# Two-block transformer kernel on one core: four taps of the first convolution done before the attention's scores, its channel mean inside the attention, its norm in chunks

## The chip, the cores and the metric

The kernel runs on one core of one Trainium2 chip. The metric is the device time of one execution in microseconds. Each kernel is timed in several executions, and the median of them is given. One further execution was recorded by the hardware profiler, and all rows below come from that one.

## The reference, cut to what matters

The program computes two transformer blocks over 256 tokens of width 1024, batch 1, in fp32. The first block begins with a mixer: an attention with 8 heads of 64 beside a convolution branch over 512 channels. The change is in that convolution branch.

```python
def conformer_conv(a, g, conv_w, conv_b, ln_g, ln_b):
    u = a * jax.nn.sigmoid(g)
    u = depthwise_conv(u, conv_w, width=31, padding=15) + conv_b   # 31 taps for each channel
    u = layernorm(u, ln_g, ln_b)                                   # over the 512 channels
    return jax.nn.silu(u)

att = dilated_sliding_attention(q, k, v)                           # 8 heads
h = h + concatenate([att, conv], axis=-1) @ w_out                  # 1024 x 1024
```

Behind it, and untouched by the change, come a cross attention, an MLP, and the two layers of the second block with a mixture of experts at the end.

## The kernel before, in words

Everything is written per engine, with semaphores between the engines. `after("name", i)` gives the semaphore value at which a named instruction has finished, and `do(..., "name", i)` marks it. Each engine runs its own list in order, so an instruction that waits holds up everything behind it on that engine.

Matrix products are made of fp32r pieces. Every fp32 operand is split into a high part (a rounded copy) and a low part (the rest), and `matmul3` issues three matmuls for each product (lines 538, 539 and 540 of the profile). Weights come in slots of 1 MB: SyncE loads a slot (three raw buffers), ScalarE writes its high part in two halves (`high`, L1461), VectorE its low part in two halves (`low`, L1983), and TensorE then uses it. There are two split buffers, so `high` of slot j waits until TensorE is done with slot j-2, and the load of slot j waits until `low` of slot j-3 is done.

The first attention is a software pipeline over steps s = 0 to 9. In step s TensorE computes the scores of head s (L758), transposes the probabilities of head s-1 (L652), multiplies those of head s-2 by the values (L672), and then does a piece of other work, `between(s)`. That piece is `cross_values(s)` for s below 8: 12 matmuls of 512 columns for the cross attention's values. VectorE in step s scales and masks the scores (L2267), takes the maximum (L2270), waits for ScalarE's exponentials, takes a reciprocal, does `low` in the even steps, and splits the attention output of a pair of heads (`outs1`, L1988 and L1990) in steps 3, 5, 7 and 9.

VectorE also computes the convolution, tap by tap, in the gaps. The 512 channels lie as four chunks of 128 x 256 in the tile C (all in the tile that the profile calls arena). `conv_taps(n)` does n pairs: a pair is one tap for two chunks, so two instructions of 128x256 (L2188). There are 62 pairs in all; the calls stop by themselves once 62 are done. 38 of them are done before the call `conv_taps(1)` that stands just ahead of the attention's loop on VectorE.

After the last tap, TensorE sums C over the channels by matmuls with a matrix of ones (`mean_over_channels`, L768; four fp32 matmuls, which the profile counts as eight), VectorE subtracts the mean (`conv_mean`, L2242), ScalarE squares (L1616), TensorE sums the squares (L768 again), VectorE scales (L2247), ScalarE takes the root (L1618), VectorE takes the reciprocal and multiplies (L2252, L2254), ScalarE applies SiLU (L1622), and VectorE splits the result (`conv_split`, L1988 and L1990).

The product with `w_out` has four slots, called wout0 to wout3 here. The first two need only the attention's four 128-row pieces of the joined input (k = 0 to 3), the last two the convolution's (k = 4 to 7). The order on TensorE after the attention is: channel mean, half of wout0, sum of squares, the other half of wout0, wout1, then a wait for the whole convolution result (`convT`), then wout2 and wout3. Transposes of the new residual and the cross attention's query projection follow.

Of the kernel before, what the change touches and what calls it, by code (L numbers as in the profile page):

```python
# [137 lines left out]
def program(nc, A, out, points, stop):  # L138
    ctx = ExitStack()
    with ctx:  # L140
# [180 lines left out]
        def col(name, i=0):  # L321
            return COL[:, COLS[name] + i:COLS[name] + i + 1]
# [55 lines left out]
        def after(*name):  # L378

            key, n = points.get(name, ("pe", 1))  # L380
            return sems[key], n
# [139 lines left out]
        with nc.Block() as block:  # L521
# [3 lines left out]
            def _(pe):  # L525
# [16 lines left out]
                def open_bank(*name):  # L542

                    k = len(order)
                    if k >= 4:
                        pe.wait_ge(*after("read", *order[k - 4]))
                    order.append(name)
                    bank_of[name] = RING_BANK[k % 4]
                    return RING_BANK[k % 4]
# [183 lines left out]
                features_out("xk", MT, "xk", 3)  # L733
                pe.wait_ge(*after("read", "qkT", 3))
                pe.wait_ge(*after("read", "v", 0, 1))
                cross_slot = {}

                def cross_values(s):
                    if s >= 8:
                        return  # L740
                    i, r, t = s // 4, s // 2 % 2, s % 2
                    if t == 0:
                        cross_slot[i, r] = weights("xv")
                    j, w = cross_slot[i, r]
                    ps = open_bank("xv", i, t) if r == 0 else bank_of["xv", i, t]
                    for k in range(4):
                        mm = matmul3(ps[:, :], lambda z: MT[:, z, 4 * r + k, t * P:(t + 1) * P],
                                     lambda z: w[:, z, k, :], r == 0 and k == 0, r == 1 and k == 3)
                    if r == 1:
                        mm.then_inc(*cpe.mark("filled", "xv", i, t))  # L750
                        cpe.also("slot", j)
                    elif t == 1:
                        mm.then_inc(*cpe.mark("slot", j))
# [7 lines left out]

                attention(0, AH, scores1, pair_outs("att_o", (), V), between=cross_values)

                def mean_over_channels(name, need, src):
                    pe.wait_ge(*after(need))
                    ps = open_bank(name)
                    for k in range(4):
                        mm = pe.matmul(ps[:, 0:S], ones, src[:, k, :], start=(k == 0), stop=(k == 3))  # L768
                    mm.then_inc(*cpe.mark("filled", name))

                for c in range(2):
                    for t in range(TT):
                        bank_of[("wout", c, t)] = banks[2 * t + c]
# [6 lines left out]
                                         lambda z: w[:, z, k % 4, :], first and k == ks[0], last and k == ks[-1])  # L780
                    return mm

                mean_over_channels("cmean", "conv", C)
                pe.wait_ge(*after("scores_read", AH - 1))
                pe.wait_ge(*after("pt_copied", AH - 1))
                pe.wait_ge(*after("read", "att_o", 3))
# [3 lines left out]
                mixed_rows(0, w, (0, 1, 2, 3), (1,), first=True).then_inc(*cpe.mark("slot", j))  # L790
                j, w = weights("wout")
                mixed_rows(1, w, (0, 1, 2, 3), (0, 1), first=True).then_inc(*cpe.mark("slot", j))
                pe.wait_ge(*after("convT"))
                for c in range(2):
                    j, w = weights("wout")
                    for t in range(TT):
                        if c == 1 and t == 1:
                            first_half_raw(2)
                        mixed_rows(c, w, (4, 5, 6, 7), (t,), last=True).then_inc(*cpe.mark("filled", "wout", c, t))
                    cpe.also("slot", j)  # L800

                features_out_raw("xq", 2, "xq", 0)
# [614 lines left out]
            def _(act):  # L1417
# [20 lines left out]
                def do(ins, *name):  # L1438
                    ins.then_inc(*cact.mark(*name))
# [176 lines left out]
                do(act.activation(SIG[:, :, :], C[:, :, :], ACT.Square), "csq")  # L1616
                act.wait_ge(*after("read", "cvar"))
                do(act.activation(U[:, 0, 0:S], U[:, 0, 0:S], ACT.Sqrt), "csd")  # L1618
                high(1)
                act.wait_ge(*after("cnormed"))  # L1620
                for i in range(4):
                    do(act.activation(C[:, i, :], C[:, i, :], ACT.Silu, bias=col("conv_ln_b", i),  # L1622
                                      scale=col("conv_ln_g", i)), "csilu")
                high(1)
                sum_deferred(2, 2, 0)
                def query(i):
# [333 lines left out]
            def _(dve):  # L1960
                def do(ins, *name):
                    ins.then_inc(*cdve.mark(*name))
# [287 lines left out]
                def conv_scaled():  # L2250
                    dve.wait_ge(*after("csd"))
                    do(dve.reciprocal(U[:, 1, 0:S], U[:, 0, 0:S]))  # L2252
                    own()
                    do(dve.tensor_tensor(C[:, :, :], C[:, :, :],  # L2254
                                         U[:, 1, 0:S].unsqueeze(1).broadcast_to([P, 4, S]), ALU.mult), "cnormed")

                def conv_split():
                    dve.wait_ge(*after("csilu"))
                    split(lambda z: CAT[:, z, 4:8, :], C[:, :, :], "convT")

                conv_taps(1)
                for s in range(AH + 2):
                    if s < AH:
                        dve.wait_ge(*after("scores", s))
# [8 lines left out]
                        do(dve.reciprocal(RDEN[:, s % 3, :], DEN[:, s % 3, :]), "rden", s)  # L2273
                    if s in (0, 2, 4, 6, 8):
                        low(1)
                    if s >= 3 and s % 2:
                        outs1(s - 2)
                    conv_taps(2 if s % 2 else 1)
                assert taps_done == [TAPS, TAPS]
                conv_mean()  # L2280
                conv_variance()
                conv_scaled()
                low(1)
# [609 lines left out]
```

## Time and profile before

| | before |
|---|---|
| median of 3 timed runs | 1460.79 us (1459.87 to 1461.65) |
| the profiled execution's own time | 1454.22 us |
| span in the profile | 1452.2 us |
| mean granted TensorE clock | 0.991 |
| TensorE matmul busy | 1387.2 us (96%) |
| VectorE busy | 1080.0 us (74%) |
| ScalarE busy | 840.2 us (58%) |

Times in the rows are counted from the start of the span. Positions such as "at 157.80" are such times. The profiled execution took 2.0 us more than its span, and it was shorter than the median of the timed runs by 6.6 us.

### The profile page before, as it was taken

What the parts mean: (1) busy time and instruction counts of PE and PEld (TensorE: products, weight loads), DVE (VectorE), ACT (ScalarE), POOL (GpSimd) and SP (SyncE); (2) the same over time, 40 slices, a digit from 0 to 9 for tenths busy, and PEclk for the clock granted to TensorE, in tenths of its full rate; (3) what the DMA queues carried; (4) which work ended last, traced back from release to release, by engine and by line L of the source; (5) the groups of instructions that cost most, each with busy time, mean ns of one, the idle gap of its engine ahead of it and who ended that gap; (6) DMA issues with size and microseconds to landing.
All of it is one profiled execution on the core that took longest, in us unless ns stands there. A gap on an engine that the chain in (4) does not pass through costs nothing.

```text
span 1452.2 us, 21919 instructions
## 1 busy us (share of the span) xinstructions
PE 1387.2 (96%) x8180; PEld 1212.3 (83%) x8180; DVE 1080.0 (74%) x1560; ACT 840.2 (58%) x1173; POOL 56.2 (4%) x60
## 2 busy tenths in 40 slices
PE   6999899999999989999999998999999999999997
PEld 6786697999988977899999997777888888888885
DVE  4988666655658887655556888677898898898896
ACT  4546453443436844444334484446788787787784
POOL 0000000000001130000000012010000000000000
PEclk9999999999999999999999999998999999999999
DMA  8642343565654501455555440119998998998982
GB/s 301 207 146 87 100 148 103 173 200 178 197 178 132 175 30 49 126 174 190 188 181 177 144 153 30 59 44 350 362 385 301 336 355 297 358 336 306 378 314 111
DMA packets 162963, 292.75 MB, mean 202 GB/s; under 512 B 6832, under 2 KB 78924, under 8 KB 162764
## 3 DMA queue, kind: packets, MB, share of 16 engines
q1 hardware_dynamic: 162336, 291.08, 57.9%
q8 instruction: 50, 0.82, 0.2%
q10 hardware_dynamic: 556, 0.67, 0.1%
q14 instruction: 21, 0.17, 0.0%
HBM read 290.69 MB, written 1.05 MB: 201 GB/s over the span
## 4 chain that ended last, share of the span: by engine, by line
PE 85%; DVE 9%; ACT 3%; issue 1%; SPq 1%; DMA 1%; POOL 0%; DVEq 0%; ACTq 0%; POOLq 0%
PE bank L538 24%; PE bank L540 24%; PE bank L539 24%; DVE weights_split L1983 3%; PE bank L1232 2%; PE bank L1035 1%; PE bank L1307 1%; PE bank L1041 1%; PE bank L1026 1%; ACT weights_split L1461 1%; PE bank L672 1%; PE bank L652 1%; PE bank L1053 1%; PE bank L1284 1%; SPq L1378 1%
## 5 line engine op out<-in xcount | busy, mean ns | idle before, releaser
L1983 DVE TENSOR_TENSOR weights_split<-weights,weights_split 128x1024 fp32r<-128x1024 f32 (+4 forms) x266 | 304.3, 1186 | 168.6 <-ACT weights_split L1461 168.4
L1461 ACT ACTIVATE weights_split<-weights 128x1024 fp32r<-128x1024 f32 (+4 forms) x266 | 258.4, 1022 | 265.0 <-PE bank L540 260.2
L538 PE MATMUL bank<-features_split,weights_split 128*128 128x256 f32 x912 | 262.6, 288 | 15.9 <-DVE weights_split L1983 5.5
L539 PE MATMUL bank<-features_split,weights_split 128*128 128x256 f32 x912 | 260.0, 285 | 0.0
L540 PE MATMUL bank<-features_split,weights_split 128*128 128x256 f32 x912 | 259.9, 285 | 0.0
L538 PE MATMUL bank<-weights_split,features_split 128*128 128x512 f32 (+3 forms) x560 | 216.9, 387 | 8.6 <-DVE features_split L1990 3.9
L540 PE MATMUL bank<-weights_split,features_split 128*128 128x512 f32 (+3 forms) x560 | 212.9, 380 | 0.0
L539 PE MATMUL bank<-weights_split,features_split 128*128 128x512 f32 (+3 forms) x560 | 212.7, 380 | 0.0
L538 PEld LDWEIGHTS bank<-features_split,weights_split 128*128 128x128 f32 x912 | 176.9, 194 | 19.8 <-DVE weights_split L1983 7.2
L539 PEld LDWEIGHTS bank<-features_split,weights_split 128*128 128x128 f32 x912 | 177.1, 194 | 0.5
L540 PEld LDWEIGHTS bank<-features_split,weights_split 128*128 128x128 f32 x912 | 176.9, 194 | 0.0
L538 PE MATMUL bank<-weights_split,hidden_split 128*128 128x512 f32 x376 | 149.0, 396 | 0.0
L540 PE MATMUL bank<-weights_split,hidden_split 128*128 128x512 f32 x376 | 146.7, 390 | 0.0
L539 PE MATMUL bank<-weights_split,hidden_split 128*128 128x512 f32 x376 | 146.5, 390 | 0.0
L538 PEld LDWEIGHTS bank<-weights_split,features_split 128*128 128x128 f32 x560 | 106.0, 189 | 27.3 <-DVE features_split L1990 4.7
L540 PEld LDWEIGHTS bank<-weights_split,features_split 128*128 128x128 f32 x560 | 105.7, 189 | 17.8
L539 PEld LDWEIGHTS bank<-weights_split,features_split 128*128 128x128 f32 x560 | 106.0, 189 | 16.7
L2807 DVE TENSOR_TENSOR weights_split<-weights,weights_split 128x1024 fp32r<-128x1024 f32 x96 | 114.8, 1221 | 3.4 <-ACT weights_split L1848 2.5
L1848 ACT ACTIVATE weights_split<-weights 128x1024 fp32r<-128x1024 f32 x96 | 100.5, 1058 | 22.7 <-PE bank L540 22.0
L538 PEld LDWEIGHTS bank<-weights_split,hidden_split 128*128 128x128 f32 x376 | 70.7, 188 | 16.3 <-issue 1.5
L540 PEld LDWEIGHTS bank<-weights_split,hidden_split 128*128 128x128 f32 x376 | 70.6, 188 | 15.3
L539 PEld LDWEIGHTS bank<-weights_split,hidden_split 128*128 128x128 f32 x376 | 70.7, 188 | 13.6
(387 smaller groups left out, 2250.5 us busy)
## 6 DMA issues: line engine op xcount, KB each, us to landing
weights<-in_moe_gate_dram SPq DMA_DIRECT2D x26, 1024.0 KB, 6.7
weights<-in_moe_up_dram SPq DMA_DIRECT2D x24, 1024.0 KB, 7.0
weights<-in_moe_down_dram SPq DMA_DIRECT2D x24, 1024.0 KB, 7.1
weights<-in_w_in_dram SPq DMA_DIRECT2D x20, 1024.0 KB, 5.1
weights<-in_w_up_dram SPq DMA_DIRECT2D x16, 1024.0 KB, 5.2
weights<-in_w_down_dram SPq DMA_DIRECT2D x16, 1024.0 KB, 4.9
weights<-in_w_out_dram SPq DMA_DIRECT2D x12, 1024.0 KB, 5.0
weights<-in_ffn_gate_dram SPq DMA_DIRECT2D x11, 1024.0 KB, 5.3
```

The source lines that it names most:

```text
L538: pe.matmul(ps, lhs(0), rhs(0), start=start, stop=False, skip_group_check=shared)
L539: pe.matmul(ps, lhs(0), rhs(1), start=False, stop=False, skip_group_check=shared)
L540: return pe.matmul(ps, lhs(1), rhs(0), start=False, stop=stop, skip_group_check=shared)
L652: mm = pe.transpose(ps[:, at:at + P], pr[:, kt * P:(kt + 1) * P], ident)
L672: mm = pe.matmul(ps[o:o + HD, first:S], v[:, kt, h * HD:(h + 1) * HD], flat(pt)[:, kt * S:(kt + 1) * S - first], start=(kt == 0), stop=(kt ...
L1026: mm = pe.matmul(inplace(ps[:, i * P:(i + 1) * P].unsqueeze(1), lev), LT[:, p, :], chosen(DI, p, 1, lev), start=True, stop=True)
L1035: mm = pe.matmul(ps[:, i * P:(i + 1) * P], DITC[:, p, :], PM[:, p, :], start=True, stop=True)
L1232: mm = pe.matmul(ps[:, k * P:(k + 1) * P], XS[:, z, t, f * P:(f + 1) * P], GSEL[:, t, :], start=(t == 0), stop=(t == TT - 1))
L1461: do(act.activation(split_flat(j)[:, 0, part], raw_flat(j)[:, part], ACT.Copy), "hi", j, b)
L1848: do(act.activation(split_flat(j)[:, 0, part], raw_flat(j)[:, part], ACT.Copy), "hi_item", s, b)
L1983: do(dve.tensor_tensor(split_flat(j)[:, 1, part], raw_flat(j)[:, part], split_flat(j)[:, 0, part].bitcast(F32), ALU.subtract), "lo", j)
L2807: do(dve.tensor_tensor(split_flat(j)[:, 1, part], raw_flat(j)[:, part], split_flat(j)[:, 0, part].bitcast(F32), ALU.subtract), "lo_item", ...
```

## The change

Four things are changed.

1. VectorE does four pairs of taps instead of one ahead of the attention loop, and two instead of one at the end of step 0. The last pair of taps now falls in step 7; before, steps 8 and 9 had one and two pairs.
2. TensorE's channel mean moves from behind the attention into step 8, behind the value product of head 6. VectorE's `conv_mean` moves into step 9, ahead of the split of the last pair of heads.
3. ScalarE gets one more activation, a SiLU of one column, behind the root. VectorE's multiplication by the reciprocal is done in four instructions of 128x256 instead of one of 128x1024, and each SiLU waits for its own chunk.
4. The split of the convolution result is done in two halves, and TensorE waits for the first half ahead of k = 4, 5 and for the second ahead of k = 6, 7.

```diff
+                def mean_over_channels(name, need, src):
+                    pe.wait_ge(*after(need))
+                    ps = open_bank(name)
+                    for k in range(4):
+                        mm = pe.matmul(ps[:, 0:S], ones, src[:, k, :], start=(k == 0), stop=(k == 3))
+                    mm.then_inc(*cpe.mark("filled", name))
+
                 def cross_values(s):
+                    if s == 8:
+                        mean_over_channels("cmean", "conv", C)
                     if s >= 8:
                         return
...
-                mean_over_channels("cmean", "conv", C)
                 pe.wait_ge(*after("scores_read", AH - 1))
...
-                pe.wait_ge(*after("convT"))
                 for c in range(2):
                     j, w = weights("wout")
                     for t in range(TT):
                         if c == 1 and t == 1:
                             first_half_raw(2)
-                        mixed_rows(c, w, (4, 5, 6, 7), (t,), last=True).then_inc(*cpe.mark("filled", "wout", c, t))
+                        pe.wait_ge(*after("convT", 0))
+                        mixed_rows(c, w, (4, 5), (t,))
+                        pe.wait_ge(*after("convT", 1))
+                        mixed_rows(c, w, (6, 7), (t,), last=True).then_inc(*cpe.mark("filled", "wout", c, t))
...
                 do(act.activation(U[:, 0, 0:S], U[:, 0, 0:S], ACT.Sqrt), "csd")
+                do(act.activation(SM[:, 15, 0:1], NHALF[:, 0:1], ACT.Silu))
                 high(1)
-                act.wait_ge(*after("cnormed"))
                 for i in range(4):
+                    act.wait_ge(*after("cnormed", i))
                     do(act.activation(C[:, i, :], C[:, i, :], ACT.Silu, bias=col("conv_ln_b", i),
-                                      scale=col("conv_ln_g", i)), "csilu")
+                                      scale=col("conv_ln_g", i)), "csilu", i)
...
-                    do(dve.tensor_tensor(C[:, :, :], C[:, :, :],
-                                         U[:, 1, 0:S].unsqueeze(1).broadcast_to([P, 4, S]), ALU.mult), "cnormed")
+                    for i in range(4):
+                        do(dve.tensor_tensor(C[:, i, :], C[:, i, :], U[:, 1, 0:S], ALU.mult), "cnormed", i)
 
                 def conv_split():
-                    dve.wait_ge(*after("csilu"))
-                    split(lambda z: CAT[:, z, 4:8, :], C[:, :, :], "convT")
-
-                conv_taps(1)
+                    for p in range(2):
+                        dve.wait_ge(*after("csilu", 2 * p + 1))
+                        split(lambda z: CAT[:, z, 4 + 2 * p:6 + 2 * p, :], C[:, 2 * p:2 * p + 2, :], "convT", p)
+
+                conv_taps(4)
                 for s in range(AH + 2):
...
+                    if s == AH + 1:
+                        conv_mean()
                     if s >= 3 and s % 2:
                         outs1(s - 2)
-                    conv_taps(2 if s % 2 else 1)
+                    conv_taps(2 if s % 2 or s == 0 else 1)
                 assert taps_done == [TAPS, TAPS]
-                conv_mean()
                 conv_variance()
```

## Rows read from the trace of the kernel before

**Rows 1.** The page: TensorE's busy time, and engines' shares of the chain that ended last.

```profile
PE 1387.2 (96%) x8180; PEld 1212.3 (83%) x8180; DVE 1080.0 (74%) x1560; ACT 840.2 (58%) x1173; POOL 56.2 (4%) x60
...
PE 85%; DVE 9%; ACT 3%; issue 1%; SPq 1%; DMA 1%; POOL 0%; DVEq 0%; ACTq 0%; POOLq 0%
```

**Rows 2.** TensorE's waits from 100 to 230: in total, times, longest, us.

```profile
PE bank L768 <- DVE arena L2188: 3.1, 1, 3.1
PE bank L538 <- DVE features_split L1990: 2.4, 1, 2.4
...
PE bank L672 <- ACT probsT L1529: 1.2, 1, 1.2
```

**Rows 3.** The chain that ended last, 104 to 200: start, length, what.

```profile
151.13 1.07 ACT weights_split L1461
152.22 2.36 DVE weights_split L1983 x2
154.59 0.79 DVE arena L2188 x2
155.38 0.34 DVE features_split L1988
155.75 0.42 DVE features_split L1990
156.17 1.59 DVE arena L2188 x4
157.80 2.88 PE bank L768 x8
...
164.18 1.73 PE bank L768 x8
...
169.04 2.01 ACT weights_split L1461 x2
171.07 1.28 ACT L1622
172.37 2.09 ACT arena L1622 x4
...
175.21 1.24 DVE features_split L1990
176.49 0.50 PE bank L538
```

**Rows 4.** VectorE in order of time; in brackets the idle time before.

```profile
100.85 4.05 DVE L2188 SCALAR_TENSOR_TENSOR arena<-arena,vector_cols 128x256 f32<-128x256 f32 x10
107.68 0.69 DVE L2267 SCALAR_TENSOR_TENSOR probs<-bank,shape_table 128x512 f32<-128x512 f32 x1 [2.77 <-PE bank L758]
...
114.68 0.68 DVE L2267 SCALAR_TENSOR_TENSOR probs<-bank,shape_table 128x512 f32<-128x512 f32 x1
...
160.72 1.23 DVE L2242 SCALAR_TENSOR_TENSOR arena<-bank,arena 128x1024 f32<-128x1024 f32 x1 [2.97 <-PE bank L768]
...
166.85 1.75 DVE L2252 RECIPROCAL arena<-arena 128x256 f32<-128x256 f32 x1 [0.48 <-ACT arena L1618]
```

**Rows 5.** TensorE in order of time, same columns.

```profile
118.40 0.66 PE L652 MATMUL bank<-shape_table,probs 128*128 128x128 f32 x4 [1.23 <-ACT probs L1535]
...
153.67 1.08 PE L672 MATMUL bank<-probsT,arena 128*64 128x256 f32 x4 [1.19 <-ACT probsT L1529]
```

**Rows 6.** Stretches: length, busy time of PE, PEld, DVE, ACT, POOL; granted clock, DMA share, GB/s.

```profile
158.90:162.10 3.20, 3.20 (x9) 2.55 (x8) 1.23 (x1) 0.12 (x1) 0.00 (x0) 0.50 0.03 12
...
165.90:168.72 2.82, 2.82 (x14) 2.29 (x13) 2.26 (x3) 0.42 (x1) 0.00 (x0) 1.00 0.00 0
173.90:176.49 2.59, 0.21 (x2) 0.01 (x1) 1.98 (x3) 2.44 (x4) 0.00 (x0) 1.00 0.99 341
```

**Rows 7.** ScalarE in order of time, around the root.

```profile
163.06 1.28 ACT L1618 ACT_TABLE_LOAD   x1
166.40 0.42 ACT L1618 ACTIVATE arena<-arena 128x256 f32<-128x256 f32 x1 [2.06 <-DVE arena L2247]
```

More of the change, by code:

```diff
@@ L762, in _ @@
                 attention(0, AH, scores1, pair_outs("att_o", (), V), between=cross_values)
[L764 to L769, printed above, removed]
                 for c in range(2):
```

## The prediction

> **What bounds the kernel now.** I read the page first, then TensorE's waits, then the chain that ended last, and then each engine in order of time around the change. TensorE's matmuls are busy for 96% of the span and 85% of the chain lies on TensorE [rows 1], so an edit pays only by the idle time of TensorE that it removes, or by a stretch that TensorE runs at a lower clock. The list of its waits names what is to be had where the convolution meets the attention: 3.1 us ahead of the channel mean (L768, waiting for the last tap), 2.4 us ahead of the second half of the `w_out` product (L538, waiting for the split of the convolution result), and 1.2 us ahead of the last value product (L672) [rows 2]. The chain shows the same place: it leaves TensorE at 151.13, goes over ScalarE's and VectorE's weight split, taps, a split, taps, comes back at 157.80, and leaves again from 169.04 to 176.49 [rows 3]. Third, the clock: from 158.90 to 162.10 it is granted at 0.50, that is 1.2 GHz in place of 2.4, after TensorE had idled 1.2 us, worked about 1 us and idled 3 us; the idle 2.4 us ahead of 176.49 left it at 1.00 [rows 2, 5, 6].
>
> **The moved taps.** A pair costs 0.79 us (two instructions) [rows 3]. Three pairs go ahead of the loop: 3 x 0.79 = 2.37 us. VectorE idles 2.77 us there for the first scores [rows 4], so they are hidden, with 0.40 us left. If that cover were gone they would cost what lies above it, 2.37 us at most. The fourth pair goes to the end of step 0, directly ahead of the scaling of the second scores at 114.68, which waits for nothing [rows 4]. That scaling releases the maximum, the exponentials and the probabilities for which TensorE idles 1.23 us at 118.40 [rows 5]. So it is on the path: plus 0.79. From there to the last value products TensorE has no wait in its list, so it carries the 0.79 along (ScalarE's `high`, whose slot TensorE frees, too) until 151.13 becomes 151.92. In exchange step 7 ends after one pair in place of two: 62 - 42 pairs are left for the loop, steps 0 to 6 take 3+3+2+3+2+3+2 = 18, and step 7 the last two. The last tap ends at 151.65, about where the first of step 7's two final pairs, moved by 0.79, lies.
>
> **The chain from 151.13 to the first `w_out` product.** Before: `low` until 154.59, one pair 0.79, the split of the last heads 0.34 + 0.42, two pairs 1.59, and TensorE's mean 2.88: the product starts at 160.68 [rows 3]. After: `low` ends 0.79 later, 155.38. Then `conv_mean`, 1.23 us alone [rows 4], about 1.15 as a step of a full queue: 156.55. Then the split of the last heads, 0.8: 157.35, and the product starts at 157.4. TensorE's mean must be ready by 155.38: its value product of head 6 ended at 153.67 - 1.19 = 152.5 [rows 5], now 153.3; the taps are done since 151.65; the mean takes 1.73 at full clock [rows 3], until 155.0. That leaves 0.4 us. The last value product (1.08 [rows 5]) then runs until 156.1, and TensorE idles 1.3 us in place of 1.2 + 3.1. Gain: 160.68 - 157.4 = 3.3 us, with the 0.79 already paid.
>
> **The clock.** Half of wout0, the sum of squares and the other half took until 168.72, 8.04 us. At full clock the second half is 2.82 us [rows 6], the first then 2.9, the sum of squares 1.73 [rows 3]: 7.45. I take full clock, since the longest idle time is now 1.3 us, and 2.4 us left the clock alone [rows 2, 6]. The gain is 0.6 us; were the clock at half as before, it would be nothing. wout0 is free at 164.9.
>
> **The second wait.** TensorE then has wout1, 168.72 to 176.49 - 2.38 = 174.1, 5.4 us: until 170.3. Everything for wout2 must be there by then. ScalarE's `high` starts 0.32 us after the slot is free [rows 3]: 165.2 to 167.25. The SiLU's table load, 1.28 us now between `high` and SiLU [rows 3], moves up behind the root, as the root's own load already lies ahead of its wait [rows 7]. The root ends near 163.05, load and one-column activation at about 164.6 (no row has that activation; between nothing and the 0.42 of the root [rows 7], I take 0.2): hidden in the wait for wout0's slot. If not hidden, at most 1.7 us. The reciprocal (1.75 [rows 4]) ends at 164.85. Four multiplications of 128x256: the nearest row is the pair's 0.79, 0.40 each and 1.6 in all, against 1.23 for one of a 128x1024 instruction [rows 3, 4]; bounds 1.2 and 1.9; they end at 166.5. Then `low` of wout2, 2.36 us [rows 3], until 168.9. The first two SiLUs, 0.52 each [rows 3], are done at 168.3. The first half split: a copy and a subtraction of 128x512. The subtraction lies between half of 1.24 and 1.24 [rows 3], and I take the 0.69 of the 128x512 instruction at 107.68 [rows 4]; the copy lies between 0.37 and 0.75 (172.37 + 2.09 to 175.21 is the whole one [rows 3]), and I take 0.42: 170.05. TensorE wants it at 170.3, so 0.2 to 0.3 us are left, and with both upper bounds it would wait 0.6 us. The second half is done near 171.2 and is wanted 6 matmuls later, at 171.7. So the wait of 2.4 us goes. wout3's `high` starts when wout1 is free, its `low` ends near 174.1, and it is wanted at 175.8. VectorE adds the first `w_out` result about 1 us later than TensorE makes it, but TensorE needs that only behind wout3's first three quarters.
>
> The Trainium skill ("ScalarE: Activation LUTs", "What ACT_TABLE_LOAD costs") gives 1.28 us for the load and another 1.38 us of drain with each switch. By its 2.66 us the one-column SiLU would end near 165.9 and `high` start 0.7 us later, which would leave TensorE waiting some 0.2 us and make the gain 6.0 us. The row with the load is followed 0.02 us after its end by the SiLU [rows 3], so I see no such drain in this trace and count none.
>
> **Sum.** 3.3 + 0.6 + 2.4 = 6.3, less 0.1 for the handovers: 6.2 us. No DMA is added or moved by itself; SyncE's loads follow VectorE's `low`, which comes earlier or keeps its distance to TensorE. Behind 176.49 all engines follow TensorE, and no wait for a load of weights is in its list [rows 2], so the 6.2 us should last. Span 1452.2 - 6.2 = 1446.0, own time of a profiled execution 1454.22 - 6.2 = 1448.0. The median of the runs stands 6.6 us above the profiled execution, and I take the same difference off it: 1460.79 - 6.2 = 1454.6 us, 0.42% less.
>
> **The rivals.**
> 1. *The path is as above* (72%). 1454.6 us; with the bounds above and the clock of other executions, 1453.4 to 1456.5. It may be that the timed executions of before don't all have the half-clock stretch: then the mean cost 1.73 and not 2.88 there, the 0.6 isn't gained either, and 6.2 - 1.15 - 0.6 = 4.5 us are left: 1456.3.
> 2. *The clock falls somewhere else* (13%). The idle time at 118.40 grows from 1.23 to 2.0 us, and about 1 us lies shortly ahead of it [rows 5]; and all later stalls come 6 us sooner, so the clock may fall at others. A stretch like the one at 158.90 costs half of its 3.2 us [rows 6], 1.6 us. One or two of them: 1456.2 to 1457.8. Against it: only the 3 us stall shows a fall here. The Trainium skill ("TensorE: Matmul & The Clock Gate", "Part 1: The HAM clock gate") says that an idle array is put at half rate and that sustained work lifts it; where in time the fall comes it leaves open, and this trace agrees with one fall and one return.
> 3. *The handover isn't gained* (11%): the mean is moved, but the halves come late, or later stages swallow the time. If the second wait stays and only the first goes, 3.3 + 0.6 = 3.9 us; if a later stage bound by something other than TensorE takes back half of all, 3.1 us; with one clock fall on top, 1.5 to 2.3 us: 1458.5 to 1460. For it: two margins of 0.2 to 0.4 us. Against it: missing them costs tenths.
> 4. *Slower* (4%). After the longer idle time at 118.40 the clock goes to half and the attention's mix of transposes and short products doesn't lift it. Each 3.2 us at half cost 1.6 us [rows 6], so to lose 6.2 + 2.9 us it must stay at half for 18 us, to about 137; until 151 it would cost 16 us: 1460.8 - 6.2 + 16 = 1470.6. Against it: the same mix kept the clock at 1.00 behind two idle times of 1.2 us, and the fall at 158.90 was over in 3.2 us.
>
> **How the numbers follow.** About 0.2% (2.9 us) is what a measurement of this kernel can tell from no change. Case 1, case 2 but for a tail, and a small part of case 3 give faster by more than that: 85%. Most of case 3 and the tail of case 2 give within 0.2%: 11%. Case 4 gives slower: 4%. The range reaches from 1452.8 (a clock fall fewer downstream, 1.6 us) to 1457.8 (case 2's end).
>
> **What the profile of the changed kernel would show.** VectorE's idle time ahead of 107.7 is 0.4 us in place of 2.77. TensorE's idle time at the second transposes is 2.0 us. The mean (L768's eight) starts directly behind the value product of head 6, near 153.3, and takes 1.7 us. The 3.1 us wait is gone, and one of about 1.3 us ends with L1990 ahead of the first `w_out` product, near 157.4. The clock is 1.00 from 150 to 176. The SiLU's table load stands near 163, ahead of `high`. The second half of the product starts near 170.3 without a wait. The prediction is wrong if the second half waits for the first split by a microsecond or more, if the clock falls between 118 and 165, or if the distance between the two traces shrinks behind 176.

## The result, and the profile after

The changed kernel took 1451.6 us in the median of 8 runs (1449.08 to 1457.93), the kernel before 1460.76 us in the same comparison (1459.87 to 1463.63). The ratio is 0.9934, with an interval from 0.9917 to 0.9952: faster by 9.2 us, 0.6%. The forecast was faster by 6.2 us, 1454.6, with a range from 1452.8 to 1457.8. So the direction was right, and the time lies 1.2 us below the range.

The profiled execution of the changed kernel has a span of 1449.0 us, only 3.2 us less than the 1452.2 of before. So the two profiles differ by 3.2, the medians by 9.2, and the forecast said 6.2. Most of this section and the experiments are about these three numbers.

TensorE's waits in the changed kernel, from 90 to 235 (in total, times, longest):

```profile
PE bank L652 <- ACT probs L1538: 3.0, 2, 2.0
PE bank L538 <- DVE features_split L1994: 2.9, 2, 1.5
PE bank L652 <- DVE probs L2105: 1.9, 2, 1.1
```

The waits of 3.1 us (mean) and 1.2 us (last value product) of [rows 2] are gone. The 2.4 us ahead of the second half are gone too. The two waits for a split that the second row counts are one of 1.5 us near 229, which the kernel before has as well (near 232), and a new one of 1.35 us ahead of the first `w_out` product, for the split of the last heads. TensorE in order of time shows it, with the idle time in brackets:

```profile
120.95 0.66 PE L652 MATMUL bank<-shape_table,probs 128*128 128x128 f32 x4 [2.02 <-ACT probs L1538]
121.53 1.96 PE L672 MATMUL bank<-probsT,arena 128*64 128x256 f32 x4
...
156.54 1.99 PE L740 MATMUL bank<-arena,shape_table 128*128 128x256 f32 x8
158.47 1.08 PE L672 MATMUL bank<-probsT,arena 128*64 128x256 f32 x4
160.90 0.47 PE L538 MATMUL bank<-weights_split,features_split 128*128 128x512 f32 x1 [1.35 <-DVE features_split L1994]
...
163.74 1.89 PE L740 MATMUL bank<-arena,shape_table 128*128 128x256 f32 x8
```

The idle time at the second transposes is 2.02 us, against 1.23 in [rows 5]: the pair at the end of step 0. The mean stands behind the value product of head 6 and holds TensorE for 1.9 us (156.54 to 158.47); in [rows 3] its own length was 2.88, here it is 1.99. No wait lies between 160.90 and the second half, which starts at 173.68.

VectorE and ScalarE around the root, in order of time:

```profile
103.79 5.23 DVE L2192 SCALAR_TENSOR_TENSOR arena<-arena,vector_cols 128x256 f32<-128x256 f32 x13
109.43 0.69 DVE L2272 SCALAR_TENSOR_TENSOR probs<-bank,shape_table 128x512 f32<-128x512 f32 x1 [0.41 <-PE bank L767]
...
158.63 1.22 DVE L2246 SCALAR_TENSOR_TENSOR arena<-bank,arena 128x1024 f32<-128x1024 f32 x1
...
168.37 1.44 DVE L2259 TENSOR_TENSOR arena<-arena 128x256 f32<-128x256 f32 x4
169.72 2.36 DVE L1987 TENSOR_TENSOR weights_split<-weights,weights_split 128x1024 fp32r<-128x1024 f32 x2
171.99 0.43 DVE L1992 CAST features_split<-arena 128x512 fp32r<-128x512 f32 x1
172.45 0.69 DVE L1994 TENSOR_TENSOR features_split<-arena,features_split 128x512 fp32r<-128x512 f32 x1
```

```profile
166.13 0.42 ACT L1621 ACTIVATE arena<-arena 128x256 f32<-128x256 f32 x1 [3.89 <-DVE arena L2251]
166.57 1.28 ACT L1622 ACT_TABLE_LOAD   x1
167.86 0.20 ACT L1622 ACTIVATE small<-minus_half 128x1 f32<-128x1 f32 x1
168.50 2.01 ACT L1464 ACTIVATE weights_split<-weights 128x1024 fp32r<-128x1024 f32 x2 [0.43 <-PE bank L540]
170.42 2.06 ACT L1626 ACTIVATE arena<-arena,vector_cols 128x256 f32<-128x256 f32 x4
```

The idle time ahead of the first scores fell from 2.77 us [rows 4] to 0.41. The table load stands ahead of the weight split, and 0.43 us are left behind it. The first half split ends at 173.1, 0.5 us before TensorE takes it. VectorE's subtraction of the mean (158.63) begins 0.1 us behind the end of TensorE's mean (156.54 + 1.99 = 158.53).

So why only 3.2 us between the two profiles? The stage from the first scores to the second half lasted 69.98 us before (106.51 to 176.49) and 65.41 after (108.27 to 173.68). That is 4.6 us less, not 6.2, and the stage began 1.8 us later, in code that the change hardly touches. Each row below gives a stretch, its length, the busy times of TensorE (matmuls, weight loads), VectorE, ScalarE and GpSimd, and then the granted clock (third number from the end). After:

```profile
108.27:173.68 65.41, 61.02 (x258) 42.78 (x257) 51.45 (x97) 42.00 (x83) 0.00 (x0) 0.97 0.25 82
...
150.00:173.68 23.68, 22.33 (x100) 16.76 (x99) 16.29 (x29) 14.29 (x23) 0.00 (x0) 1.00 0.29 91
```

and three stretches of 10 us that were at 1.00 in the first profile of before. The last row is that profile's own 120 to 130:

```profile
10.00:20.00 10.00, 4.88 (x26) 4.91 (x27) 6.42 (x10) 6.50 (x10) 0.70 (x1) 0.66 1.06 410
...
60.00:70.00 10.00, 7.43 (x36) 5.80 (x35) 10.00 (x16) 4.55 (x6) 0.00 (x0) 0.85 0.49 158
...
120.00:130.00 10.00, 9.05 (x33) 5.69 (x34) 8.52 (x17) 6.05 (x13) 0.00 (x0) 0.83 0.22 66
...
120.00:130.00 10.00, 10.00 (x44) 6.94 (x44) 8.90 (x20) 6.67 (x18) 0.00 (x0) 1.00 0.34 106
```

In this execution the clock fell to 1.2 GHz near 10, near 65, and near 120, behind the longer idle time at the second transposes, but not between 150 and 174. Below, such a stretch at 1.2 GHz is called a fall. The fall near 120 costs the missing 1.6 us of the stage: the four value matmuls at 121.53 took 1.96 us in place of 1.08, and those behind it were slow too. The falls ahead of the stage cost less: the clock was at 0.94 over those 108 us, against 1.00 over the 107 us of before, and the stage began only 1.8 us later.

### The profile page after: what moved, and what is told of

It is laid out like the page before. It is cut to its first block, busy times and chain, and to the rows that moved or that the text cites. A ratio compares the mean times of both kernels' runs of the same rounds, so it can differ in the third digit from the quotient of the medians.

```text
span 1449.0 us, 21926 instructions
## 1 busy us (share of the span) xinstructions
PE 1389.6 (96%) x8180; PEld 1214.3 (84%) x8180; DVE 1080.0 (75%) x1565; ACT 840.2 (58%) x1174; POOL 56.1 (4%) x60
## 4 chain that ended last, share of the span: by engine, by line
PE 86%; DVE 9%; ACT 3%; issue 1%; DMA 0%; POOL 0%; DVEq 0%; SPq 0%; ACTq 0%
PE bank L538 25%; PE bank L540 24%; PE bank L539 24%; DVE weights_split L1987 3%; PE bank L1235 2%; PE bank L1038 1%; PE bank L1310 1%; PE bank L1044 1%; PE bank L1029 1%; ACT weights_split L1464 1%; PE bank L672 1%; PE bank L652 1%; PE bank L1056 1%; PE bank L1287 1%; DVE arena L2557 1%
```

## The experiments

"Theory A" in the expectations is that of the forecast: three handovers on TensorE's path, each worth what its rows say, and the clock drawn anew in each execution. "Stage" is the time from the first scores (the first matmul from `arena`, 64*128) to the first matmul of the second half. The runs of before_filled_stall, before_delay_5p5, delay_5p5_again and no_early_table were made on another chip than those of the other experiments. The kernel before had a median of 1460.8 us there, and of 1461.3 and 1461.2 us in the two comparisons on the other chip.

| kernel | timed median (runs) | ratio, interval | mean clock of the timed runs | stage in its profile | clock in the stage |
|---|---|---|---|---|---|
| before, in the three comparisons of the experiments | 1461.3 (110) | | 0.9830 | 69.98; 70.01 | 0.98; 0.98 |
| changed | 1451.6 (8) | 0.9934, 0.9917 to 0.9952 | 0.9869 | 65.41 | 0.97 |
| after_again | 1453.01 (12) | 0.9952, 0.9935 to 0.9969 | 0.9852 | 63.82 | 1.00 |
| norm_edits_only | 1463.0 (12) | 1.0012, 0.9990 to 1.0033 | 0.9800 | 67.46 | 0.97 |
| taps_mean_only | 1462.4 (12) | 0.9997, 0.9974 to 1.0019 | 0.9821 | 69.31 | 0.95 |
| delay_2p7 | 1456.56 (12) | 0.9984, 0.9955 to 1.0013 | 0.9840 | 66.54 | 1.00 |
| delay_5p5 | 1467.09 (12) | 1.0032, 1.0008 to 1.0057 | 0.9805 | 70.86 | 0.98 |
| delay_5p5_again | 1461.44 (12) | 1.0009, 0.9989 to 1.0029 | 0.9848 | 69.25 | 1.00 |
| no_step0_pair | 1452.54 (8) | 0.9944, 0.9925 to 0.9963 | 0.9852 | 63.03 | 1.00 |
| first_heads_first | 1452.35 (11) | 0.9944, 0.9925 to 0.9963 | 0.9835 | 61.63 | 1.00 |
| before_filled_stall | 1459.58 (12) | 0.9994, 0.9975 to 1.0013 | 0.9838 | 68.30 | 1.00 |
| before_delay_5p5 | 1462.5 (12) | 1.0017, 0.9998 to 1.0035 | 0.9842 | 72.90 | 0.98 |
| no_early_table | 1455.36 (12) | 0.9958, 0.9941 to 0.9974 | 0.9853 | 64.67 | 1.00 |

**before_again.** No edit.

> The kernel before, unchanged, to see what a usual execution of it looks like: its timed runs stand 6.6 us above the one profiled execution. Theory A (the granted clock): the new profile has more stretches at 1.2 GHz than the first one, its mean granted clock is nearer 0.985 than 0.991, and its span is near 1458 us, with the same waits ahead of the channel mean (3 us) and the second half of the w_out product (2.4 us). Theory B (something else in the path): the clock is about 0.991 again, and a wait or a start-up stretch is longer. Timed ratio to before: 1.000 within 0.2%.

The median was 1461.62 us (12 runs, ratio 0.9995). The span was 1457.9 at a mean clock of 0.986, so theory A's picture held: the first profile of before (1452.2 at 0.991) was one of the quick executions. The stage is the same to 0.03 us, with the same waits. What differs lies behind it, in the clock. From 920 to 950, in the first profile of before and then in this one:

```profile
920.00:950.00 30.00, 28.47 (x209) 24.63 (x208) 19.97 (x42) 12.97 (x26) 2.66 (x2) 1.00 0.26 89
```

```profile
106.61:176.62 70.01, 61.12 (x258) 42.98 (x257) 53.31 (x97) 43.66 (x84) 0.00 (x0) 0.98 0.27 88
920.00:950.00 30.00, 28.47 (x203) 25.49 (x203) 17.34 (x39) 12.18 (x27) 1.33 (x1) 0.89 0.20 71
```

**after_again.** No edit.

> The changed kernel, unchanged, beside the kernel before on the same chip. Theory A: again some 8 to 9 us below before (ratio 0.994), of which about 6 us lie between the first scores and the second half of the w_out product and the rest in clock stretches elsewhere, which differ from execution to execution by several us. Theory B: the same difference in every execution, and a stage behind 200 us that is shorter by 3 us at the same granted clock.

In this profile no fall lies in the stage, and the stage lasts 63.82 us: 6.2 us less than before, to the tenth what the sum said. The span is 1457.9 all the same, for the clock was at half for more than half of the 30 us from 920 to 950:

```profile
106.62:170.44 63.82, 59.42 (x258) 41.94 (x257) 51.29 (x97) 41.85 (x83) 0.00 (x0) 1.00 0.25 84
...
920.00:950.00 30.00, 28.47 (x164) 24.39 (x163) 14.15 (x32) 9.08 (x19) 1.33 (x1) 0.72 0.20 71
```

The median is 8.3 us below before, as theory A said. Theory B (a later stage shorter at the same clock) finds nothing: the rest of the program, from the second half on, took 1275.7 and 1281.3 us in the two profiles of before and 1275.3 and 1287.5 in those of the changed kernel. The time lost in it to the clock (length times one less granted clock, summed over stretches of 10 us) was 11.9, 18.3, 11.7 and 26.5 us, in the same order.

**norm_edits_only.** The early table load, the chunks and the halves, without the moved taps and mean:

```diff
-                    if s == 8:
-                        mean_over_channels("cmean", "conv", C)
...
+                mean_over_channels("cmean", "conv", C)
                 pe.wait_ge(*after("scores_read", AH - 1))
...
-                conv_taps(4)
+                conv_taps(1)
...
-                    if s == AH + 1:
-                        conv_mean()
...
-                    conv_taps(2 if s % 2 or s == 0 else 1)
+                    conv_taps(2 if s % 2 else 1)
                 assert taps_done == [TAPS, TAPS]
+                conv_mean()
```

> Only the early SiLU table load, the chunked multiplication, and the split in halves; taps and mean as before. Theory A (two separate handovers): the 2.4 us wait ahead of the second half goes, the 3.1 us wait stays: 2 to 2.6 us faster than before, 1458.3. Rival (the clock decides): with the 3 us wait still there the half-clock stretch stays, but removing the second wait also saves one fall in executions in which it starts one, then up to 4 us. Rival (no gain): the wait stays at 1 us or more since the table load isn't hidden: 1 us or less.

The stage lasted 67.46 us, 2.5 less; the 3.1 us wait and a fall at 158 stayed. The wait ahead of the second half is gone from the list (the 1.5 us are the one far behind it, of which before has its own):

```profile
PE bank L740 <- DVE arena L2191: 3.1, 1, 3.1
PE bank L652 <- ACT probs L1537: 2.3, 2, 1.2
...
PE bank L538 <- DVE features_split L1993: 1.5, 1, 1.5
```

But the timed median, forecast at 1458.3, is no better than before: 1463.0. Its mean clock is the lowest of all, 0.980.

**taps_mean_only.** The other two parts:

```diff
-                        pe.wait_ge(*after("convT", 0))
-                        mixed_rows(c, w, (4, 5), (t,))
                         pe.wait_ge(*after("convT", 1))
-                        mixed_rows(c, w, (6, 7), (t,), last=True)...
+                        mixed_rows(c, w, (4, 5, 6, 7), (t,), last=True)...
...
-                do(act.activation(SM[:, 15, 0:1], NHALF[:, 0:1], ACT.Silu))
...
```

The multiplication is one instruction again, every SiLU waits for it, and the split is one piece.

> Only the moved taps and the channel mean in step 8; norm, SiLU and split as before. Theory A: the first handover gives 3.3 us and the clock at the mean 0.6 us, and the second wait of 2.4 us stays: 3.9 us faster than before, 1456.9. Rival (the clock decides): it gives nearly all of the change, 6 to 9 us, since the stall of 3 us is what lets the clock fall in this stage, and the other edits give nearly nothing.

The first handover goes and the wait of 2.5 us stays. The stage came out at 69.31. The clock was at half in two places where it isn't in before:

```profile
118.20:125.00 6.80, 4.78 (x14) 2.68 (x13) 5.74 (x14) 5.76 (x14) 0.00 (x0) 0.66 0.33 127
176.20:179.60 3.40, 1.93 (x6) 1.63 (x7) 3.37 (x4) 1.23 (x2) 0.00 (x0) 0.83 0.54 190
```

```profile
177.67 0.47 PE L538 MATMUL bank<-weights_split,features_split 128*128 128x512 f32 x1 [2.48 <-DVE features_split L1991]
```

The first lasts from 120 to 127, 6.8 us, as long as two of the falls elsewhere (3.4 us each), and costs the stage some 3.3 us. The second begins near 178.4, behind the 2.48 us wait, and so lies outside the stage. With the first taken out the stage is 66.0 us, 2.3 less than the 68.3 of before without its fall. The rows gave 2.15: 3.3 less the 1.15 that the fall had added to the mean.

The rival, that this part alone gives nearly all, is refuted by the median, 1462.4; so is theory A's 1456.9. By the medians neither part alone gives anything, and both together 8 to 9 us. By the stages without falls they are 2.5 and 2.3 us, and both together 4.5. That called for the next four.

**delay_2p7 and delay_5p5.** Half, or all, of wout1's products computed once more (the expectation below says a quarter, but wout1 has 24 matmuls and takes 5.4 us):

```diff
+                mixed_rows(1, w, (0, 1, 2, 3), (0,), first=True, last=True)     # delay_2p7; (0, 1) in delay_5p5
                 mixed_rows(1, w, (0, 1, 2, 3), (0, 1), first=True).then_inc(*cpe.mark("slot", j))
```

> The changed kernel with 12 matmuls of 512 columns more (a quarter of wout1's products is computed twice), so that TensorE works 2.73 us longer ahead of the second half and everything behind comes later, with no stall added. Theory A (the time lost at 1.2 GHz is drawn anew in each execution and has nothing to do with where the stage ends): 2.7 us slower than the changed kernel, 1455.2. Theory C (the place of the later stalls in time decides how many falls there are): a difference that isn't 2.7 us, between 0 and 7, and a mean granted clock that differs from the changed kernel's 0.986 by 0.003 or more.

> The same with 24 matmuls, 5.46 us, so that the later stages start nearly where they start in the kernel before. Theory A: 5.5 us slower than the changed kernel, 1458.0, still 3 us faster than before, since this stage's own clock falls stay away. Theory C: equal to before, 1461, with the mean granted clock of before, 0.982 to 0.983.

The stages: 66.54 without a fall, 2.72 more than 63.82, and 70.86 with one. The medians: 3.6 us and 14.1 us above after_again. The first is within 1 us of theory A (its mean clock, 0.9840, is 0.002 below the changed kernel's, where theory C asked for 0.003), the second is not: 5.5 us of work cost 14. Theory C's numbers for it (1461, a clock of 0.982 to 0.983) are missed too: 1467.1 at 0.9805. Three of delay_2p7's runs took 1469 us, so its mean lies further off than its median.

**delay_5p5_again.** The same kernel once more, in another comparison and on the other chip.

> The same kernel as delay_5p5, in another job. It came out 14 us above the changed kernel where 5.5 us of work were added. If the excess belongs to this kernel (theory C), it is there again: 1465 to 1469. If it belongs to the job (the phase in which its executions happened to start), the median is nearer 1458 and the mean clock nearer 0.986.

Now 1461.4 at a mean clock of 0.985, where it had been 1467.1 at 0.9805. Neither forecast fits: it lies between them. Of the 8.6 us beyond the added work 3 were there again, so more than half of the excess does not belong to the kernel. Whether it belongs to the chip or to the draw of the clock can't be told from these runs; the kernel before had nearly the same median on both chips.

**no_step0_pair.**

```diff
-                    conv_taps(2 if s % 2 or s == 0 else 1)
+                    conv_taps(2 if s % 2 else 1)
```

> The changed kernel without the pair at the end of step 0. Theory A: TensorE's idle time ahead of the second transposes is 1.23 us again, the stage from the first scores to the second half lasts 63.0 us in place of 63.8, and no fall of the clock comes in the attention: 0.8 us faster than the changed kernel, up to 1.5 with the falls saved, 1451 to 1451.7. Rival: the pair's cost was hidden, no difference, stage 63.8.

The stage lasts 63.03 us, 0.79 less, and the wait at the second transposes is 1.2 us again. The median shows nothing of it (1452.54 against 1453.01 and 1451.6).

**first_heads_first.** The edit of no_step0_pair, and

```diff
-                pe.wait_ge(*after("read", "att_o", 3))
                 j, w = weights("wout")
-                mixed_rows(0, w, (0, 1, 2, 3), (0,), first=True)
+                mixed_rows(0, w, (0, 1, 2), (0,), first=True)
+                pe.wait_ge(*after("read", "att_o", 3))
+                mixed_rows(0, w, (3,), (0,))
```

> The same, and the first w_out product begins with the rows of heads 0 to 5, and waits for the last pair of heads only ahead of its last quarter. Theory A: the 1.35 us wait ahead of the first product goes, the stage lasts 61.7 us, 2.1 us less than in the changed kernel: 1450.4. Rival: the second half then waits for the split of the convolution result (0.5 us of margin in the changed kernel) and 0.5 us or more of it comes back.

The stage lasts 61.63 us, 2.2 less than in the changed kernel, and of the waits between 90 and 180 these are left:

```profile
PE bank L652 <- ACT probs L1539: 2.3, 2, 1.2
PE bank L730 <- ACT arena L1516: 1.3, 1, 1.3
```

It has the shortest path of all. Its median, forecast at 1450.4, is level with the changed kernel's (1452.35 against 1451.6 and 1453.01), at a lower mean clock (0.9835 against 0.9869 and 0.9852).

**before_filled_stall.** In the kernel before, ahead of the wait for the last tap:

```diff
                 def mean_over_channels(name, need, src):
-                    pe.wait_ge(*after(need))
                     ps = open_bank(name)
+                    for _ in range(6 if name == "cmean" else 0):
+                        pe.matmul(ps[:, 0:S], ones, upper_ones, start=True, stop=True)
+                    pe.wait_ge(*after(need))
```

> The kernel before with six fp32 matmuls of 256 columns on the constant tables (2.6 us, into the bank that the channel mean opens anyway) ahead of the wait for the last tap, so that TensorE isn't idle there; the wait's end doesn't move. Theory A (the 3 us stall is what lets the clock fall): no half-rate stretch at 156, the stage from the first scores to the second half lasts 68.3 us in place of 70.0, and the median is 1.7 us below before, 1459.6. Rival: the clock falls there all the same, stage 70.0. Theory C (later falls follow from where the later stages lie): the stage as in A, but a median off by several us either way.

```profile
156.93 2.86 PE L767 MATMUL bank<-shape_table 128*128 128x256 f32 x12
160.05 1.99 PE L770 MATMUL bank<-arena,shape_table 128*128 128x256 f32 x8 [0.27 <-DVE arena L2190]
...
177.07 0.79 PE L538 MATMUL bank<-weights_split,features_split 128*128 128x512 f32 x1 [2.38 <-DVE features_split L1992]
```

```profile
150.00:170.00 20.00, 18.54 (x83) 14.14 (x81) 13.20 (x24) 8.60 (x15) 0.00 (x0) 1.00 0.28 104
174.40:177.80 3.40, 1.02 (x4) 0.63 (x3) 2.70 (x3) 2.52 (x4) 0.00 (x0) 0.84 0.88 304
```

The idle time is gone (0.27 us are left of 3.05), the clock stays up through the mean, and the stage lasts 68.30 us: 1.7 us less for work whose result is overwritten. So the stall let the clock fall, and the fall cost 1.7 us. All four profiles that have this stall have the fall behind it, and this one has neither.

But here the clock fell at the next idle time, the 2.38 us ahead of the second half (its first matmul takes 0.79 us, against 0.50 in [rows 3]), which in both profiles of before had left it alone. That fall lies just behind the end of the stage. The cross attention's first transposes that wait (L652) stand 46.6 to 46.8 us behind the start of the second half in every profile without a fall there. Here it is 48.2 us, and 48.3 in taps_mean_only, where the clock fell behind the same wait. So from the first scores to those transposes before_filled_stall gains only 0.3 us (116.5 against 116.7), and the changed kernel 6.3 (110.4). The median says the same: 0.9994.

The two handovers may therefore not be independent. Where the clock had fallen at 158, the wait of 2.4 us left it alone (2 of 2 profiles); where it had not, it fell there (2 of 2). Only both edits together remove both. That the second fall comes because the first is gone is argued from four profiles and not shown.

**before_delay_5p5.** The 24 extra matmuls in the kernel before.

> The kernel before with 24 more matmuls in wout1 (5.46 us). In it, the second half already waits 2.4 us for the convolution result, so 2.4 us of the delay are hidden: the stage should last 73.1 us. Theory A: 3.1 us slower than before, 1464.4. Theory C: off from that by several us, with the mean granted clock off from 0.983 by the matching amount (0.001 of clock stood for 1.1 us over the runs so far).

The stage lasts 72.90 us, 2.9 more: of 5.5 us of added work, 2.4 went into the wait ahead of the second half, which is gone from its list. The median is 1.7 us above before; theory A said 3.1.

**no_early_table.** The changed kernel without the line with the one-column SiLU.

> The changed kernel without the one-column SiLU, so that the table load (1.28 us) lies between the weight split and the first SiLU again. Theory A: the margin of 0.5 us ahead of the second half is used up and TensorE waits 0.8 us, so the stage lasts 64.6 us in place of 63.8; the median 0.8 us above the changed kernel, which the runs can't tell from the clock's spread. Rival: the load stays hidden behind VectorE's weight split, stage 63.8.

```profile
167.46 1.28 ACT L1625 ACT_TABLE_LOAD   x1
168.76 2.08 ACT L1625 ACTIVATE arena<-arena,vector_cols 128x256 f32<-128x256 f32 x4
```

```profile
171.19 0.47 PE L538 MATMUL bank<-weights_split,features_split 128*128 128x512 f32 x1 [0.69 <-DVE features_split L1993]
```

TensorE waits 0.69 us ahead of the second half, and the stage lasts 64.67 us, 0.85 more. So the margin of 0.5 us was real, and the early load is worth what the load exceeds it by. The median is 1455.36, 2.4 us above after_again's and 3.8 above the changed kernel's first, of which the stage explains 0.85; as the expectation said, the runs don't resolve that.

## Where the prediction was right, and where it was wrong

**The path was right, term by term.** With the stage as the measure, and the one profile of the changed kernel without a fall in it:

- All in all, 6.2 us: 70.0 to 63.82. As predicted.
- The moved taps: three pairs hidden with 0.40 us left (0.41), the fourth 0.79 us on the path. Taking it away gave 0.79.
- The first handover: the product starts 51.03 us behind the first scores in after_again (157.65 less 106.62). Predicted were 157.4 less 106.51, 50.9.
- The clock at the mean: 1.7 us, of which 1.15 was counted in the mean's 2.88 and 0.6 apart. The filled stall gave 1.7 within the stage.
- TensorE's mean: it took 1.99 us at full clock and not 1.73, so of the 0.4 us of margin ahead of VectorE's subtraction 0.1 was left.
- The second handover: 2.4 predicted, 2.5 when made alone.
- The table load: hidden. The Trainium skill ("ScalarE: Activation LUTs", "What ACT_TABLE_LOAD costs") has 1.28 us for the load and 1.38 of drain. The row at 166.57 agrees with the first, and the SiLU at 167.86 stands 0.01 us behind the load's end, so no drain is seen. The margin at the second half was 0.5 us, not 0.2 to 0.3: the four multiplications took 1.44 us, and I had 1.6.

**The step that failed is the last of the sum:** "I take the same difference off it". It takes the path's 6.2 us off the median, as if the clock outside the stage were the same for both kernels. The term that was mis-sized is this clock: the sum puts it at nothing, and the range at one fall of 1.6 us. The timed runs of the changed kernel had a mean clock of 0.9869 (0.9852 in after_again), those of before 0.9830. Worked out below, the 0.0039 between them go with 4.0 us, of which the forecast had the 1.7 of the fall at 158. And the fixed distance of 6.6 us between the profiled execution and the median isn't there: the profiled execution lay 1.7 us below the median in before_again, 0.4 below for the changed kernel, and 7.0 above in after_again. The 6.6 us were mostly clock: 0.991 in the first profile of before, 0.983 on average in its timed runs. Single runs of before lie between 1454 and 1469 us, those of delay_5p5 between 1458 and 1473. That the direction came out does not rest on luck, since the path alone gives it; that the clock outside the stage would add 2 us and more to it was not foreseen.

How far this explains the 9.2 us can be worked out from the timed runs, since each has its mean granted clock. I laid one straight line with a common slope through all 245 of them, with a level of its own for each kernel. The slope is 0.70 us for each us of "span times (1 less clock)", so 0.001 of mean clock goes with 1.0 us, and what is left over scatters by 1.8 us. (The eight runs of before in the first comparison came without their clocks and are not among them.) The levels are at equal clock, with their 95% interval, against the stages with the falls taken out at 1.6 to 1.7 us each (68.3 for before):

| kernel | stage against before's 68.3 | timed, at equal clock |
|---|---|---|
| changed | -4.5 | -5.2 +- 0.9 |
| norm_edits_only | -2.5 | -2.8 +- 1.1 |
| taps_mean_only | -2.3 | -1.2 +- 1.1 |
| delay_2p7 | -1.8 | -1.2 +- 1.1 |
| delay_5p5; again | +0.9 | +2.4; +2.1 +- 1.1 |
| no_step0_pair | -5.3 | -6.1 +- 1.3 |
| first_heads_first | -6.7 | -7.7 +- 1.1 |
| before_filled_stall | 0 | -1.0 +- 1.1 |
| before_delay_5p5 | +2.9 | +3.3 +- 1.1 |
| no_early_table | -3.6 | -3.7 +- 1.1 |

Once the clock is set equal, the timed runs follow the path; the largest gap is 1.5 us, in delay_5p5. Some 0.7 us of it lie outside the span: the timed run is 2.7 to 2.8 us longer than its span in the kernels with 24 extra matmuls, and 2.1 us in before.

For the changed kernel that leaves -5.2 us. In the first comparison its clock was 0.0039 higher, and 0.0039 times 1460 times 0.70 is another -4.0: together the 9.2 us measured. In after_again it is 0.0022 and -2.2: together 7.4, where the means differ by 7.4 and the medians by 8.3. This is no independent test, since the same runs went into the line. The forecast had 6.2 of the 9.2: 4.5 of path at full clock and the 1.7 of the fall. Of the 3.0 that it lacked, 2.3 are clock outside the stage and 0.7 the distance from -4.5 to -5.2, which is within what is uncertain. That is what put the time below the range.

**The signs of being wrong** that the forecast named: the second half did not wait. The clock did fall between 118 and 165 in the first profile, near 121, and cost 1.6 us; in the second it did not. The distance between the traces did not shrink behind 176 in the first pair of profiles (2.8 us at the second half, 3.2 at the end), and went from 6.2 us to nothing in the second pair, which the clock took back.

**The rivals.** A part of rival 2 came true in the first profile: the clock fell behind the 2.02 us at the second transposes. In the second profile, with the same idle time, it did not. Over all kernels with that idle time it fell in 3 of 7 profiles. Rival 4 is refuted: of the 10 us from 120 to 130, at 0.83, some 3.4 us were at half, and the rest of the attention was at full clock. The longest stretch at half behind that idle time, in taps_mean_only, took 6.8 us. Rival 3 is refuted by the stages.

**What stays open.** Why the timed runs of the changed kernel have the higher mean clock beyond the fall removed, and why norm_edits_only has the lowest; no run shows a cause for either. That the place of the later stalls in time matters was a theory (C) that the two delays could not settle: against after_again's median 2.7 us cost 3.6, and 5.5 us cost 14 once and 8.4 the second time, on the other chip. The same kernel's mean clock differed by 0.004 between the two, as much as between most kernels here. So about 2 to 3 us of the 9.2 may not be there in other executions; after_again found 8.3.

## What to carry to other kernels

A profile is one draw. Where TensorE sets the end and has idle times of 1 to 3 us, compare a stage between two fixed instructions, best in two profiles of each kernel, and with the granted clock beside it: here that resolved 0.8 us, while medians of 12 runs could not tell 2.5 us from nothing. Look a few microseconds past the end of the stage too: of the 1.7 us that the filled stall gained 1.4 were lost again just behind it. Where the timed runs carry their granted clock, set it equal before reading a difference below 1%. And a product over several inputs should begin with those that are ready, and wait for the last one only ahead of its own quarter: that took away 1.35 us of waiting in this stage.

## What the runs showed of the hardware that I had not expected

- The same idle time lets the clock fall in one execution and not in another: 2.38 us ahead of the second half did not in either profile of before and did in that of before_filled_stall, as 2.48 us did in taps_mean_only; 2.02 us at the second transposes did in one profile of the changed kernel and not in the other. 3.05 us ahead of the mean did in 4 of 4.
- Matmuls on constants in a stall of 3.1 us kept the clock at 1.00 and took 1.7 us off the stage, but the clock fell at the next wait, and 1.4 us of it were gone 46 us later.
- Executions of one kernel differ by up to 19 us (delay_2p7: 1450.6 at a mean clock of 0.991, 1469.6 at 0.977), though only one core works.
- A fall cost much less in one place than in another: with the clock at 0.94 over the 108 us ahead of the stage (some 6.5 us of clock) the stage began 1.8 us later, while a fall inside the stage (1.7 us of clock) cost 1.6 to 1.7 us.
